# Loading the neighbourhood heads' first slices and weights in the tail of the first program

## The reference

```python
x = layer_norm(x, ln_in_g, ln_in_b)
proj = x @ w_in[l]
gq, gk, gv, gg, glr, nq, nk, nv = jnp.split(proj, pts, axis=-1)
o_gla = gla_mixer(gq, gk, gv, gg, glr, ...)
o_na = neighbourhood_attention(nq, nk, nv, na_rpb[l])
mix = jnp.concatenate([o_gla, o_na], axis=-1) @ w_out[l]
x = layer_norm(DEEPNORM_ALPHA * x + mix, ln1_g[l], ln1_b[l])
f = conv_gated_mlp(x, w_up[l], conv_w[l], conv_b[l], w_down[l])
x = layer_norm(DEEPNORM_ALPHA * x + f, ln2_g[l], ln2_b[l])
```

## Time and profile before

| | us |
|---|---|
| median of 3 runs | 3312.49 |
| lowest and highest | 3311.0, 3316.92 |
| the profiled execution | 3312.96 |
| its span, first to last instruction | 3311.2 |
| granted PE clock, mean of the span | 0.98 |

### The profile page before, as it was taken

The page is one execution under the profiler, slowest core; times in us unless marked ns, Lnnn a source line. Parts: engine busy times, 40 slices in busy tenths (PEclk is TensorE's granted clock), DMA queues, the critical chain, the costliest instruction groups (busy, mean ns, idle before and its releaser), DMA issues.

```text
span 3311.2 us, 42422 instructions
## 1 busy us (share of the span) xinstructions
PE 3160.8 (95%) x15664; PEld 2536.2 (77%) x15664; DVE 1782.0 (54%) x3367; ACT 1150.0 (35%) x2198; POOL 396.4 (12%) x406
## 2 busy tenths in 40 slices
PE   6999999886999978999999999999999999999997
PEld 5777767664777757888888888888888888888885
DVE  7647646754776665555735345343454434443377
ACT  2257356522444342443432232222322222222221
POOL 0012100006444400000002000110001100020000
PEclk9999999997999999999999999999999999999998
DMA  7889788858888636986877536575465753656553
GB/s 274 329 277 299 241 287 256 274 185 257 274 260 258 238 130 258 363 287 209 304 259 298 193 140 239 197 288 193 144 235 206 283 197 141 235 210 228 191 193 125
DMA packets 252173, 782.81 MB, mean 236 GB/s; under 512 B 28962, under 2 KB 95922, under 8 KB 209728
## 3 DMA queue, kind: packets, MB, share of 16 engines
q1 hardware_dynamic: 219776, 596.50, 52.6%
q10 hardware_dynamic: 19008, 138.42, 11.5%
q0 software_dynamic: 13184, 45.17, 3.9%
HBM read 605.26 MB, written 178.85 MB: 237 GB/s over the span
## 4 chain that ended last, share of the span: by engine, by line
PE 60%; DVE 2%; DMA 1%; issue 0%; ACT 0%; SPq 0%; POOL 0%; ACTq 0%; DVEq 0%
PE trunk_ps_h L76 12%; PE trunk_ps_h L78 12%; PE trunk_ps_h L77 12%; PE trunk_ps_f L76 8%; PE trunk_ps_f L78 8%; PE trunk_ps_f L77 8%; DMA trunk_raw<-in_w_out 1%; PE trunk_ps_h L2057 0%; DVE trunk_raw L1947 0%; DVE trunk_y L1807 0%; DVE trunk_y L1812 0%; DVE trunk_y L1796 0%; DVE trunk_w L1775 0%; DVE trunk_xt L1869 0%; ACT trunk_w L1686 0%
## 5 line engine op out<-in xcount | busy, mean ns | idle before, releaser
L76 PE MATMUL trunk_ps_h<-trunk_xt,trunk_w 128*128 128x512 f32 x1760 | 685.5, 389 | 2.8 <-DVE trunk_xt L1869 2.8
L77 PE MATMUL trunk_ps_h<-trunk_xt,trunk_w 128*128 128x512 f32 x1760 | 685.4, 389 | 0.0
L78 PE MATMUL trunk_ps_h<-trunk_xt,trunk_w 128*128 128x512 f32 x1760 | 685.3, 389 | 0.0
L1899 DVE SCALAR_TENSOR_TENSOR trunk_tt<-trunk_hb,trunk_cw,trunk_tt 128x512 f32<-128x512 f32 x220 | 187.0, 850 | 654.5 <-ACT trunk_tt L1716 654.5
L76 PE MATMUL trunk_ps_f<-trunk_w,trunk_m 128*128 128x512 f32 x1168 | 457.8, 392 | 13.3 <-DMA trunk_m<-mix_lo 12.4
L77 PE MATMUL trunk_ps_f<-trunk_w,trunk_m 128*128 128x512 f32 x1168 | 455.9, 390 | 0.0
L78 PE MATMUL trunk_ps_f<-trunk_w,trunk_m 128*128 128x512 f32 x1168 | 455.8, 390 | 0.0
L1714 ACT ACTIVATE trunk_hb<-trunk_ps_h 128x512 f32<-128x512 f32 x220 | 131.9, 600 | 857.9 <-PE trunk_ps_h L78 857.9
L76 PEld LDWEIGHTS trunk_ps_h<-trunk_xt,trunk_w 128*128 128x128 f32 x1760 | 330.9, 188 | 71.7 <-issue 3.2
L77 PEld LDWEIGHTS trunk_ps_h<-trunk_xt,trunk_w 128*128 128x128 f32 x1760 | 330.8, 188 | 68.9
L78 PEld LDWEIGHTS trunk_ps_h<-trunk_xt,trunk_w 128*128 128x128 f32 x1760 | 330.8, 188 | 68.9
(11 more groups left out here) (217 smaller groups left out, 4594.7 us busy)
## 6 DMA issues: line engine op xcount, KB each, us to landing
trunk_w<-wu_s SPq DMA_DIRECT2D x88, 1024.0 KB, 4.8
trunk_w<-wu_s ACTq DMA_DIRECT2D x88, 1024.0 KB, 4.8
near_xr<-xt_s SPq DMA_DIRECT2D x160, 512.0 KB, 6.4
front_xr<-xt_s SPq DMA_DIRECT2D x120, 512.0 KB, 6.4
wu_s<-trunk_w SPq DMA_DIRECT2D x44, 1024.0 KB, 4.9
trunk_w<-wd_s SPq DMA_DIRECT2D x44, 1024.0 KB, 4.8
trunk_w<-wd_s ACTq DMA_DIRECT2D x44, 1024.0 KB, 4.8
trunk_raw<-in_w_up SPq DMA_DIRECT2D x44, 512.0 KB, 5.9
```

Source lines behind the costliest of these rows:

```text
L76: pe.matmul(out, lh, rh, start=first, stop=False, skip_group_check=skip)
L77: pe.matmul(out, lh, rl, start=False, stop=False, skip_group_check=skip)
L78: return pe.matmul(out, ll, rh, start=False, stop=last, skip_group_check=skip)
L1899: dve.scalar_tensor_tensor(out, hb[:, i, s, a_j:a_j + BLK], tap[:, a_j:a_j + 1], out, ALU.mult, ALU.add).then_inc(conv_step, 1)
```

## The change

The rings of slices, split weights and raw weights of the three programs become views of two tensors that outlive them, `shared_ring` and `shared_spare`. In the tail of `project_gla`, at steps 161 to 174, SP issues the 6 slices and 8 raw weight tiles with which `natten` began; ACT and DVE split the first four tiles at steps 165, 168, 171 and 174. `natten` starts without these loads and splits, and its waits count from what lies there already. In the trace the tiles `front_xr`, `front_w`, `near_xr`, `near_w`, `near_o`, `trunk_m` and `trunk_w` are then named `shared_ring`, and the raw tiles `shared_spare`.

```diff
+RING, SPARE = 16 * D, 3 * D
+class Shared:
+    def __init__(self, nc, ctx):
+        self.ring = ctx.enter_context(nc.sbuf_tensor("shared_ring", [P, RING], F32R))
+        self.spare = ctx.enter_context(nc.sbuf_tensor("shared_spare", [P, SPARE], F32))
...
+    def near(self):
+        at = N_XRING * 2 * BLK
+        end = at + N_WRING * 4 * P
+        xr = self.ring[:, 0:at].rearrange("p (s a n) -> p s a n", s=N_XRING, a=2)
+        w = self.ring[:, at:end].rearrange("p (s a n) -> p s a n", s=N_WRING, a=2)
+        o = self.ring[:, end:end + 4 * BLK].rearrange("p (s a n) -> p s a n", s=2, a=2)
+        return xr, w, o, self.spare[:, 0:N_RAWS * 2 * P].rearrange("p (s n) -> p s n", s=N_RAWS)
...
+NEAR_W = 4
...
+        def near_split_at(n):
+            m, odd = divmod(n - NSTEP - 5, 3)
+            return [] if odd or not 0 <= m < NEAR_W else [m]
...
+            def load_near(i):
+                if i == 0:
+                    sp.wait_ge(stepped, NSTEP)
+                    sp.wait_ge(w_lo, NPASS * KC)
+                m = i // 2 if i < 2 * N_AHEAD else i - N_AHEAD
+                if i % 2 and i < 2 * N_AHEAD:
+                    sp.dma_start(near_xr[:, m].bitcast(F32), xt_s[ORDER[0], m]).then_inc(near_x_in, 16)
+                else:
+                    sp.dma_start(near_raw[:, m, :], w_pair[0, m]).then_inc(near_w_in[m], 16)
...
                 for j in at(shifted(out_step, 9), n):
                     store_mix(j)
+                if 0 <= n - NSTEP - 1 < N_AHEAD + N_RAWS:
+                    load_near(n - NSTEP - 1)
...
+            sp.wait_ge(near_x_in, 16 * N_AHEAD)
+            for m in range(N_RAWS):
+                sp.wait_ge(near_w_in[m], 16)
+            sp.wait_ge(near_w_lo, NEAR_W)
...
+            def near_split(m):
+                act.wait_ge(near_w_in[m], 16)
+                act.wait_ge(stepped, NSTEP)
+                act.activation(near_w[:, m, 0, 0:P], near_raw[:, m, 0:P], ACT.Copy, scale=DH ** -0.5)
+                act.activation(near_w[:, m, 0, P:], near_raw[:, m, P:], ACT.Copy).then_inc(near_w_hi, 1)
...
+            def near_split(m):
+                dve.wait_ge(near_w_hi, m + 1)
+                hi = near_w[:, m, 0, :].bitcast(F32)
+                dve.scalar_tensor_tensor(near_w[:, m, 1, 0:P], near_raw[:, m, 0:P], DH ** -0.5, hi[:, 0:P],
+                                         ALU.mult, ALU.subtract)
+                dve.tensor_tensor(near_w[:, m, 1, P:], near_raw[:, m, P:], hi[:, P:], ALU.subtract).then_inc(near_w_lo, 1)
...
         def splits_at(n):
-            return [m for m in range(PAIRS * KC) if split_step(m) == n]
+            return [m for m in range(NEAR_W, PAIRS * KC) if split_step(m) == n]
...
-                    sp.wait_ge(w_lo, m - N_RAWS + 1)
+                    need(sp, w_lo, m - N_RAWS + 1 - NEAR_W)
...
-            for n in range(N_AHEAD):
-                load_xt(n)
-                for m in (2 * n, 2 * n + 1):
-                    if m < N_RAWS:
-                        load_w(m)
             sp.dma_start(ident[:], ident_in).then_inc(ident_in_sbuf, 16)
...
-                act.wait_ge(w_in[m % N_RAWS], 16 * (m // N_RAWS + 1))
+                need(act, w_in[m % N_RAWS], 16 * (m // N_RAWS))
...
-                pe.wait_ge(xt_in[n % N_XRING], 16 * (n // N_XRING + 1))
+                need(pe, xt_in[n % N_XRING], 16 * (n // N_XRING + (n % N_XRING >= N_AHEAD)))
                 if n % PER_PASS < KC:
-                    pe.wait_ge(w_lo, m + 1)
+                    need(pe, w_lo, m + 1 - NEAR_W)
```

57 lines of the change are left out of this document (35 added, 22 removed).

## The result

The changed kernel takes 3316.9 us (median of 20 runs, 3313.11 to 3325.13), the kernel before 3312.43 in runs beside it (20 runs, 3306.47 to 3322.07). The ratio is 1.0016, with a 95% interval from 1.001 to 1.0022: slower, by 5 us as the ratio has it, and less than 0.2%. The profiled execution took 3316.42 us with a span of 3314.6.

What follows compares the result with a forecast made beforehand. PE is busy 95% of the span; early in natten it waits for DVE, shut out by POOL's table run. Tail +1.5 and earlier POOL start -0.5 sum to +1.0 us: 3313.5 us against the median of 3312.49, range 3295 to 3318.

Steps and rivals of the forecast that it cites:

- the gate: Early in natten: PE waits for DVE's negation of job 0's maxima, shut out until POOL's first bias table run ends; 14.56 us.
- the likeliest case: Gate stays shut, so the opening's lead is lost there; 3308 to 3318 us, chance 0.50.
- Step 1, the opening: Start of natten: without loads and splits, PE reaches step 18, job 0, about 12 us earlier.
- Step 2, the gate: PE's lead is lost waiting for DVE and POOL; only POOL's run starting earlier counts, -0.5 us, bounds -4 and +1.5.
- Step 3, the tail: End of the first program: the added loads delay its loop and last stores by 1.5 us, bounds 0 and +4.
- Step 4, the splits: First program's tail: four split pairs each on ACT and DVE fit idle times; nothing charged, 2 us without cover.
- The open gate: Rival: DVE gets in beside POOL's table and PE keeps its 12 us; 3298.0 us, between 3294 and 3303, chance 0.36.
- The tail in full: Rival: first program's loop is queue-bound, so all 10.4 us of transfers lengthen it, gate shut; 3322 us, chance 0.09.

Runs made afterwards that it cites:

- tail_alone: Changed kernel's first-program tail kept, but natten loads and splits its first slices itself as in the kernel before; 3319.1 us, ratio 1.0015.
- no_tail_loads: Changed kernel without the fourteen loads, eight splits and SP's waits for them in the tail, part of the computation left out; 3314.43 us, ratio 1.0001.
- burst_loads: Changed kernel with all fourteen loads issued in one go at the first program's step 158, splits unmoved; 3313.13 us, ratio 1.0002.
- pool_one_by_one: Changed kernel with POOL waiting for its own last addition before nearly each of the first head pair's 48; 3301.44 us, ratio 0.9965.
- pause_by_part: Changed kernel with POOL waiting for its last addition only at the three boundaries between the first table's four parts; 3308.28 us, ratio 0.9982.
- pause_once: Changed kernel with a single POOL wait for its own last addition, after 24 of the first table's 48; 3307.56 us, ratio 0.9982.

## Why the prediction was right in its number, and where its steps were off

The forecast of 3313.5 us and the measured 3316.9 are both within 0.2% of the kernel before, and the gate stayed shut as the likeliest case had it. The sum was 1.0 us, the measurement 4.5, by the ratio 5. The range went up to 3318, so the time lies in it by 1 us, with the tail above the bound that the prediction gave it: the mechanism of the gate is right by reading, the closeness of the number in part by luck.

**Step 1, the opening** was right in kind and 1.2 us too high: 10.8 us of lead instead of 12, counted from SP's first issue. The first matmul is at 757.63, 0.03 us behind SP's first issue (forecast: within 0.5), and no wait stands at steps 1 and 2. A wait of 1.89 us at 773.65 is new. The slow stretch of the clock lasts 5.3 us and not the 3.8 assumed.

**Step 2, the gate**, held: one L1344 of 25.30 us (forecast: about 26) that ends with POOL's run, and a lead that is worth nothing behind it. Its term was wrong in sign: POOL's run starts 16.2 us after its first issue, 15.8 before, so +0.4 instead of -0.5, and just outside the 15 to 16 us that were named as its sign. In the profiled executions with loads at the start of `natten` it is 15.1 to 16.7, in those without 15.8 to 16.6. So no run shows the landing of the biases to depend on them, and this term is not told from zero.

**Step 3, the tail, was the term that failed**: 1.5 us forecast with 4 as its upper bound, some 5 us measured (`tail_alone` +5, `no_tail_loads` and `burst_loads` -5 and -4.6 by their ratios). The prediction compared bytes with the free share of the queue. (SP's timeline has two slices and a tile before the load of output 18, a slice and two tiles before that of output 19.) But the loop waits for the landing of one load. In each of the seven traces with near loads among the loop's own, one of the last two K/Q loads took 4.7 to 5.8 us instead of 3.4 to 3.7. Behind such a wait, of 2.12 us in the changed kernel, PE's next matmuls ran at half clock, which the sum had no term for. Nor had it one for SP's ten fulfilled waits at the hand-over, put at nothing: 0.6 us. The last store of the profiled execution landed at 755.24, 2.3 us later than before (forecast: 1 to 2).

**Step 4, the splits**, at nothing: nothing against it. `burst_loads` has all eight of them and costs nothing.

**The rivals.** The open gate was forecast at 3298. With the gate opened by other means the changed kernel takes 3301.4, and with 3.5 us less of tail it would be at the forecast. The chance of 0.36 leaned on the view that the wait is of one instruction. The Trainium skill (SBUF — State Buffer, Who interferes with whom) says that whoever issues first has the shared ports for that whole instruction. The runs agree with it where DVE waits for about one addition: 0.69 us in `pool_one_by_one`, 1.24 in `pause_by_part`. They differ from it for a long chain without gaps, where DVE was held through 20 to 32 additions. That the trace of before spoke against the rule was the right reading. The tail in full, 3322, had a cost of twice the size and another mechanism: it took the loop to be bound by the queue's bytes and not by latency, and `burst_loads` moves the same bytes beside it without the cost.

The trace of before also had, unread, a row that would have sharpened step 2. DVE's splits there are let in at the start of POOL's run, each for about one addition:

```profile
771.98 1.13 DVE L1251 SCALAR_TENSOR_TENSOR near_w<-near_raw,near_w 128x128 fp32r<-128x128 f32 x1 [1.00 <-ACT near_w L1202]
773.03 1.09 DVE L1253 TENSOR_TENSOR near_w<-near_raw,near_w 128x128 fp32r<-128x128 f32 x1
```

That is 1 to 8 us into the run; the negation at 28 us into it was held. The splits are another kind of operation (they read two tensors in SBUF), but TENSOR_SCALARs get in as well early in the tables of the later pairs. The change moves just these splits ahead of POOL's run.

## What to carry to other kernels

When a lead upstream ends at an operation that takes some hundred times its median, find what it ends with before you build more lead: here one wait inserted into GpSimd's chain (behind the 24th of 48 additions) was worth 11 us by the ratios, and the change itself 13 us beside the kernel before with the waits of `pool_one_by_one` in both, and -5 us without them. Loads that are moved under a loop are not free because its queue has free share: here they were free where SP issued nothing that the loop was waiting for, and that is a place in the timeline, not a percentage. After each step, read which wait is next: the value loads were worth 6 us in the changed kernel, and in the kernel before 10 us of lead in the opening were lost again at weight tiles of the second pair.

## What the runs showed of the hardware

- A TENSOR_SCALAR of DVE between operands in SBUF that is asked for after a long unbroken chain of GpSimd additions, in which no such operation of DVE had got in for long, is held to the chain's end. This was seen in each of the six traces that left the chain whole: asked for 16.1 to 28.6 us into the chain, held 14.2 to 26.1 us. A gap of 0.08 us lets it in.
- Held and not held part by how long DVE had kept away. The seven operations that were held (six, and the one of 8.31 us in `pause_once`) came after 15.8 us or more in which additions ran without a gap and no TENSOR_SCALAR or split of DVE got in. The other 1240 such operations that began in an unbroken stretch of additions, in all fourteen traces, came after at most 7.4 us of that, and none took more than 1.65 us, though they were asked for up to 17.9 us into the stretch. Where between 7.4 and 15.8 us it turns, and whether by time or by the number of additions passed, stays open; no run varied this alone.
- Operations of DVE that read PSUM were not held: the additions of bias to scores (`near_s<-near_ps_s,near_table`, 0.55 us) and the evictions of q and k (0.69 us) ran beside the chain at their usual time. Nor was a reciprocal of 128x2 in SBUF (0.16 us).
- The first program's tail has a life of its own. In the profiled executions its last store lands between 752.8 and 754.6 us without near loads, and between 755.2 and 762.1 with them between the loop's own; the three latest are those in which the granted clock is 0.50 for all of the last 25 us. Late data and low clock go together there. How much each would cost alone was not separated.
